# A gate stage in which ScalarE writes the weighted one-hot rows of every eighth unit

## What is computed

```python
v1, i1 = lax.top_k(s1, PEER_TOPK)            # s1, s2: (T, 8 heads, 128 keys)
v2, i2 = lax.top_k(s2, PEER_TOPK)
...
idx = jnp.take_along_axis(cand_idx, pos, axis=-1)    # i1 * 128 + i2: 128 slots for each token
gates = jax.nn.softmax(top_s, axis=-1)
...
u = expert_down[ib]
act = jax.nn.gelu(jnp.einsum("td,thkd->thk", hb, u), approximate=False)
v = expert_up[ib]
return jnp.einsum("thk,thkd->td", gb * act, v)
```

## Time and profile before

| | |
|---|---|
| three runs | 2797.36, 2802.61, 2801.85 us; median 2801.85 |
| profiled execution, own time | 2799.06 us |
| its span, first to last instruction | 2797.4 us |
| PE busy | 2656.8 us (95%) |
| DVE busy | 1807.5 us (65%) |
| ACT busy | 943.0 us (34%) |
| POOL busy | 835.6 us (30%) |
| mean granted TensorE clock | 0.984 of full speed |

### The profile page before, as it was taken

How to read it: one execution, slowest core, us unless ns; L and a number is a source line. 1 busy time by engine, 2 the same in 40 slices (tenths; PEclk the granted TensorE clock), 3 DMA queues, 4 the chain that set the end, 5 groups by cost and what they waited for, 6 DMA issues and landing times.

```text
span 2797.4 us, 35916 instructions
## 1 busy us (share of the span) xinstructions
PE 2656.8 (95%) x12743; PEld 2116.6 (76%) x12743; DVE 1807.5 (65%) x3275; ACT 943.0 (34%) x1219; POOL 835.6 (30%) x542
## 2 busy tenths in 40 slices
PE   4999999999899999999999999999999999899997
PEld 2455445699877899999999887699877877588875
DVE  6752765799999688888888898550128532560532
ACT  2323332333477333223333222443233233332321
POOL 3100011155200144444444322243221234244442
PEclk8999999999999999999999999999999999999999
DMA  9511334333355799999999897223624432122221
GB/s 339 186 57 59 117 141 152 124 123 124 111 198 200 270 336 337 333 334 334 336 341 328 300 309 279 100 83 124 97 90 148 146 120 84 59 98 91 98 90 60
DMA packets 194570, 507.23 MB, mean 181 GB/s; under 512 B 31184, under 2 KB 83184, under 8 KB 192416
## 3 DMA queue, kind: packets, MB, share of 16 engines
q1 hardware_dynamic: 144880, 321.89, 34.6%
q0 software_dynamic: 49584, 184.04, 18.2%
HBM read 456.65 MB, written 49.22 MB: 181 GB/s over the span
## 4 chain that ended last, share of the span: by engine, by line
PE 63%; issue 16%; DVE 12%; POOL 5%; DMA 2%; ACT 1%; DVEq 1%; POOLq 0%; ACTq 0%
PE psum L1668 19%; PE psum L1970 14%; PE psum L1655 13%; PE psum L531 6%; PE psum L546 5%; POOL l_r L878 5%; DVE arena L2018 3%; DVE arena L2015 2%; DVE look_oh L2015 2%; DVE arena L2022 1%; DVEq L2018 1%; PE psum L1977 1%; PE psum L1395 1%; DVE arena L2362 1%; DVE arena L2363 1%
## 5 line engine op out<-in xcount | busy, mean ns | idle before, releaser
L903 ACT ACTIVATE arena<-psum 128x512 f32<-128x512 f32 (+8 forms) x474 | 320.5, 687 | 1102.5 <-PE psum L1655 346.6
L2015 DVE TENSOR_TENSOR arena<-arena 128x384 f32<-128x384 f32 (+8 forms) x399 | 305.7, 772 | 497.3 <-ACT arena L903 269.3
L1668 PE MATMUL psum<-e_r,e_r 128*128 128x512 f32 x2304 | 541.1, 393 | 7.8 <-DVE e_r L2015 7.8
L878 POOL TENSOR_TENSOR l_r<-arena,l_r 128x1024 fp32r<-128x1024 f32 x144 | 351.2, 2440 | 659.6 <-ACT l_r L490 659.6
L1655 PE MATMUL psum<-e_r,e_r 128*128 128x384 f32 x2048 | 534.1, 341 | 3.6 <-ACT arena L903 2.4
L1668 PEld LDWEIGHTS psum<-e_r,e_r 128*128 128x128 f32 x2304 | 434.6, 189 | 97.0 <-issue 4.6
L903 ACT ACTIVATE e_r<-arena 128x1024 fp32r<-128x1024 f32 x256 | 270.2, 1057 | 368.7 <-PE psum L1668 350.1
L1655 PEld LDWEIGHTS psum<-e_r,e_r 128*128 128x128 f32 x2048 | 365.7, 189 | 14.6 <-POOL l_r L848 6.0
L1655 PE MATMUL psum<-e_r,l_r 128*128 128x384 f32 x1024 | 344.6, 337 | 0.0
L862 POOL DMA_INDIRECT arena<-in_down_rows,arena x128 | 160.0, 1250 | 430.8 <-DMA scratch_early<-arena 193.3
L862 POOL DMA_INDIRECT arena<-in_up,arena x128 | 162.0, 1266 | 250.0 <-DVE arena L2499 122.2
(11 more groups left out here) (231 smaller groups left out, 3306.7 us busy)
## 6 DMA issues: line engine op xcount, KB each, us to landing
arena<-in_down SPq DMA_DIRECT2D x128, 512.0 KB
arena<-in_up SPq DMA_DIRECT2D x128, 512.0 KB
arena<-in_w_ada POOLq DMA_DIRECT2D x48, 512.0 KB, 6.8
scratch_gates<-arena SPq DMA_DIRECT2D x12, 2048.0 KB, 7.2
arena<-scratch_gates SPq DMA_DIRECT2D x30, 768.0 KB
arena<-in_w_in SPq DMA_DIRECT2D x44, 512.0 KB, 3.3
arena<-in_w_query SPq DMA_DIRECT2D x16, 512.0 KB, 3.3
arena<-in_w_glu SPq DMA_DIRECT2D x16, 512.0 KB, 3.2
```

Of the source, the lines that this page charges most:

```text
L878: nc.gpsimd.tensor_tensor(rr(lo, 1024, "l"), reg(RING + q % NSLOT * SLOT, 1024), rr(hi, 1024, "l").bitcast(F32), ALU.subtract).then_inc(S[ ...
L903: do(sc.activation(out, in_, f, **kw), sem)
L1668: last = mm(bank(2 * tt_ + hf), rr(w__ + tt_ * P, P), rr(x__ + hf * 512, 512), start=(first and n == 0), stop=(final and n == 2))
L2015: do(v.tensor_tensor(out, a, b, op), sem)
```

## The change

In each chunk the unit with x % 8 == 7 has its B rows written by ACT into a buffer of their own (`small`, columns 96 to 607), in place of DVE. For one token ACT needs two operations: `Abs` of (i2 - iota), and `Relu` of (gate - gate * distance), which is the gate where the distance is 0, and 0 elsewhere since the distance is at least 1 and gates are positive. ACT does one token in each of the four iterations of its loop, ahead of the two copies. The `Abs` has one pointer operand (i2) and ACT waits for its completion; the `Relu` has two (minus the gate as scale, the gate as bias) and signals the new semaphore `b_hotx`, on which PE waits in that unit in addition to what it waited for before. One Copy of 128x48 ahead of the rounds makes the negated gates (`minus_g`). DVE writes A of this unit still; the second half of its chunk is now written out, without a loop. `mag8`, which a later stage uses, moves to other columns of `small`.

```diff
--- before.py
+++ after.py
@@ -129,7 +129,7 @@
     "dve_events": [("pads", 1), ("xr", 8), ("dt_x", 1), ("a_col", 1), ("conv_acc", 12), ("xdt", 8), ("cbm", 2), ("hst", 6),
                    ("ymix", 8), ("xr2", 8), ("hsplit", 1), ("xf_ready", 8), ("gate_lin", 4), ("gd", 1),
                    ("gq", 4), ("ff_split", 32)],
-    "act_6": [("u_hi", 128), ("l_hi", 144)],
+    "act_6": [("b_hotx", 48), ("u_hi", 128), ("l_hi", 144)],
     "pool_1": [("l_lo", 144)],
     "dve_1": [("dte_x", 1), ("sc_free", 4), ("ktok", 4)],
     "dve_2": [("xdte", 3), ("mdec", 16), ("gate_x", 1), ("sm", 4)],
@@ -334,6 +334,8 @@
         assert STG[1] + 4096 <= R0 and SELX + 4 * 384 <= R0
         GB = 2
         OA, OB = UHI, UHI + GB * 512
+        OBX = 96
+        minus_g = small[:, 608:656]
         GATH = PV
         EOUT = PV
         assert GATH + NGATH * 1024 <= R0
@@ -410,7 +412,7 @@
         dtecol = small[:, 352:400]
         a_col = small[:, 400:464]
         dtx, dt_t, dt_2, dt_s = (small[:, 464 + 64 * n:528 + 64 * n] for n in range(4))
-        mag8 = small[:, 256:320]
+        mag8 = small[:, 32:96]
         g_sq, g_mid = gsc[:, 8:16], mod[:, 0:8]
 
         def wslot(s, kt, mcols=P):
@@ -1134,6 +1136,9 @@
             wait("slots_mm", 1)
             for n, at_ in enumerate((I1T, I2T, GT)):
                 act_(reg(at_, TD), bank(n, TD), ACT.Copy, "~slots_T")
+            wait("slots_T", 3)
+            act_(minus_g.rearrange("p (c t) -> p c t", c=NGC),
+                 reg(GT, TD).rearrange("p (c x t) -> p c x t", c=NGC, x=8)[:, :, 7, :], ACT.Copy, scale=-1.0)
 
 
             tn.base["g_evac"] = GB
@@ -1141,7 +1146,11 @@
                 if c >= 2:
                     wait(f"g_stored{c % 2}", 16 * (c // 2))
                 stg = reg(STG[c % 2], GCHUNK * P).rearrange("p (j t) -> p t j", j=P)
-                with tn.loop(8 // GB, g_evac=GB) as i:
+                with tn.loop(8 // GB, g_evac=GB, act_own=1, b_hotx=1) as i:
+                    hot = small[:, bass.ds(i * P + OBX, P)]
+                    act_(hot, con("iota"), ACT.Abs, scale=-1.0, bias=A[:, bass.ds(i + (I2T + 32 * c + 28), 1)])
+                    act_(hot, hot, ACT.Relu, "~b_hotx", scale=small[:, bass.ds(i + (608 + 4 * c), 1)],
+                         bias=A[:, bass.ds(i + (GT + 32 * c + 28), 1)])
                     for u_ in range(GB):
                         wait("g_mm", i * GB + (GB + c * 8 + u_ + 1))
                         act_(stg[:, bass.ds(i * (4 * GB) + 4 * u_, 4), :],
@@ -1687,9 +1696,12 @@
                     r, u_ = x // 8, x % GB
                     pe.wait_ge(S["b_hot"], S.base("b_hot") + i * (8 * NSLOT) + (x + 1))
                     pe.wait_ge(S["g_evac"], S.base("g_evac") + i * (8 * NSLOT) + (x + 1))
+                    if x % 8 == 7:
+                        pe.wait_ge(S["b_hotx"], S.base("b_hotx") + i * (4 * NSLOT) + 4 * (r + 1))
                     for t in range(4):
                         last = mm(bank(u_)[:, t * P:(t + 1) * P], reg(OA + u_ * 512 + t * P, P),
-                                  reg(OB + u_ * 512 + t * P, P), start=True, stop=True)
+                                  small[:, OBX + t * P:OBX + (t + 1) * P] if x % 8 == 7 else reg(OB + u_ * 512 + t * P, P),
+                                  start=True, stop=True)
                     last.then_inc(S["g_mm"], 1)
                     if x % 8 == 0:
                         pe.wait_ge(S["d_loB"], S.base("d_loB") + i * NSLOT + (r + 1))
@@ -2448,16 +2460,29 @@
             low_d(EB)
             wait("slots_T", 3)
             for c in range(2 * NGC):
-                with tn.loop(4 // GB, b_hot=GB) as i:
-                    for u_ in range(GB):
-                        n = 4 * c + u_
-                        wait("g_mm", i * GB + (n + 1))
+                if c % 2 == 0:
+                    with tn.loop(4 // GB, b_hot=GB) as i:
+                        for u_ in range(GB):
+                            n = 4 * c + u_
+                            wait("g_mm", i * GB + (n + 1))
+                            tt(three(OA + u_ * 512, 4, P), bc(con("iota").unsqueeze(1), [P, 4, P]),
+                               bc(A[:, bass.ds(i * (4 * GB) + (I1T + 4 * n), 4)].unsqueeze(2), [P, 4, P]), ALU.is_equal, FREE)
+                            for t in range(4):
+                                ts(reg(OB + u_ * 512 + t * P, P), con("iota"),
+                                   A[:, bass.ds(i * (4 * GB) + (I2T + 4 * n + t), 1)],
+                                   A[:, bass.ds(i * (4 * GB) + (GT + 4 * n + t), 1)], ALU.is_equal, ALU.mult,
+                                   "~b_hot" if t == 3 else FREE)
+                else:
+                    for n in range(4 * c, 4 * c + 4):
+                        u_ = n % GB
+                        wait("g_mm", n + 1)
                         tt(three(OA + u_ * 512, 4, P), bc(con("iota").unsqueeze(1), [P, 4, P]),
-                           bc(A[:, bass.ds(i * (4 * GB) + (I1T + 4 * n), 4)].unsqueeze(2), [P, 4, P]), ALU.is_equal, FREE)
-                        for t in range(4):
-                            ts(reg(OB + u_ * 512 + t * P, P), con("iota"), A[:, bass.ds(i * (4 * GB) + (I2T + 4 * n + t), 1)],
-                               A[:, bass.ds(i * (4 * GB) + (GT + 4 * n + t), 1)], ALU.is_equal, ALU.mult,
-                               "~b_hot" if t == 3 else FREE)
+                           bc(reg(I1T + 4 * n, 4).unsqueeze(2), [P, 4, P]), ALU.is_equal,
+                           "~b_hot" if n % 8 == 7 else FREE)
+                        if n % 8 < 7:
+                            for t in range(4):
+                                ts(reg(OB + u_ * 512 + t * P, P), con("iota"), reg(I2T + 4 * n + t, 1),
+                                   reg(GT + 4 * n + t, 1), ALU.is_equal, ALU.mult, "~b_hot" if t == 3 else FREE)
                 if c % 2 == 0:
                     low_d(EB + c // 2 + 1)
             for n in range(EB + ES + 1, EO):
```

## The result

The changed kernel took 2831.27 us in the median of 4 runs (2824.63 to 2837.56), the kernel before 2802.23 us (4 runs). The ratio is 1.0105, with a 95% interval of 1.0080 to 1.0131: slower by about 1%, where 2829.5 us (2812 to 2838) had been forecast. In a second set of 6 runs the ratio was 1.0079 (1.0063 to 1.0096, median 2826.45 us). The profiled execution took 2827.14 us for a span of 2825.5 us, 28.1 us more than the span of before.

A forecast was written before the change was run, and what follows sets the result against it. DVE was taken to bound the kernel before at 14.16 us per chunk, ACT afterwards at 12.41 + 4 x 1.04 + 0.14 = 16.71. That adds 29.0 us: 2828.1 profiled, 2829.5 us forecast for the median, range 2812 to 2838.

The forecast's parts named there:

- ACT's slack: Gate rounds before the change: ACT has 14.16 - 12.41 = 1.75 us to spare per chunk.
- DVE's 14.16 us per chunk: Gate rounds before the change: DVE bounds, eight units of 1.63 us and one `low_d` of 1.13 us per chunk.
- ACT's 12.41: ACT's own need per chunk before the change, in us, from start distances: 4 x 1.29 + 3 x 1.53 + 2.66.
- ACT's price: Added to each ACT iteration: one Abs and Relu pair, 1.04 us with wait and register instructions, bounds 0.71 to 1.14.
- PE's wait at unit 7: PE's matmuls of unit 7 wait for the fourth Relu, delaying ACT's copy: 0.14 us per chunk.
- The sum: ACT's chunk becomes 12.41 + 4 x 1.04 + 0.14 = 16.71 us; last copy of the rounds 29.0 us later.
- what the change removes: DVE loses four of 32 B operations per chunk, 1.02 us, and would need 13.14 us.
- the rival in which DVE's saving counts: ACT has room in the rounds, so DVE's 12 x 1.02 = 12.2 us go: 2788 us, chance 0.05.
- the point of 0.40 us: Price per Abs and Relu pair on ACT below which a gain was expected: (14.16 - 12.41 - 0.14) / 4.
- Written-out code at nothing: DVE's second half of a chunk without a loop: register instructions already hidden, so worth nothing, at most 0.093 us per operation.
- The cheap pair at 0.71 us: Rival: ACT bounds the rounds but a pair costs only 0.71 us, chunk 15.39 us, 2814 us; chance 0.10.
- fall of the clock: Rival: PE's clock falls in the rounds, half of the units at the lower level, 27 us on top, 2856 us; chance 0.08.

The follow-up runs named there:

- ACT's part alone: Kernel before plus ACT's 48 pairs of Abs and Relu and the negated gates, rows read by nobody, DVE and PE unchanged: 2826.65 us, ratio 1.0083.
- DVE's part alone: Changed kernel without ACT's Abs and Relu and PE's wait for them; PE reads zeros in every eighth unit: 2804.56 us, ratio 1.0003.
- The last two versions: Kernel before, ACT writing one token per second unit, an iteration ahead, copies without own waits: 2794.10 us (0.9972); also DVE's units written out: 2787.72 us (0.9947).
- all units written out: Kernel before, ACT writing one token per second unit an iteration ahead, copies without own waits, DVE's loops written out in both chunk halves: 2787.72 us, ratio 0.9947.
- the spread saving: Kernel before with DVE leaving out one token's B in every second unit, PE multiplying by zeros there, ACT as before: 2793.71 us, ratio 0.9957.

## Why the prediction was right, and where it was not

**The bound of before, and ACT's slack.** DVE's 14.16 us per chunk held. ACT's 12.41 was a little too much: in the chunk of 16.33 us shown above, the steps other than the pairs and the wait at unit 7 add up to 12.23. Two pairs more raise the chunk to 14.25, four to 16.33. That the slack was taken from pitches between starts and not from busy time was right: by busy time the pairs would have fitted in.

**ACT's price.** A pair was put at 1.04 us; it is 0.98 from Abs to copy, plus 0.02 in the gap ahead of it. The two operations cost what was worked out (0.39 and 0.48, measured 0.40 and 0.49); of the two 0.03 us for register instructions only the 0.02 is seen, and the wait between them is 0.18, not 0.20. The two copies of an iteration are 1.26 us apart in place of 1.29.

**PE's wait at unit 7.** 0.14 us was forecast; 1.44 - 1.26 = 0.18 us was measured, and ACT's part alone, without the wait, has the chunk shorter by 16.33 - 16.14 = 0.19.

**The sum.** The chunk was put at 16.71 and is 16.33 us (16.40 in the mean of ten), and the rounds, first copy to last, grew by (943.08 - 748.24) - (916.22 - 747.05) = 25.7 us where 29.0 was forecast. The median shows 29.0 us more and the second set 23.5 us, so the median's agreement to 2 us with the forecast is in part luck. What follows shifted and gave nothing back, as said: from the last copy's start to the end it is 1882.4 us, and was 1881.2.

**The step that was wrong** stands under "what the change removes": that DVE "would need 13.14 us", and so the price of the rival in which DVE's saving counts, 2788 us. DVE's part alone gives 14.0 us and no gain. Bunched in one unit the saving turns into a wait for the buffers; the two-deep ring (`GB` = 2) was described and not followed through. Even spread, the 13.14 was reached only once A had no register instruction behind that wait. The forecast did not rest on it only because ACT's chain was longer still. It does mean that this change, with its saving in one unit, could not have won more than about 12 x 0.15 = 1.8 us at any price of the pair (the rounds of VectorE's part alone are 1.8 us shorter), so the point of 0.40 us that the prediction gave for a gain was without meaning.

**Written-out code at nothing** was right where it stands (ratio 0.9990), and the register instructions of B are hidden as said. The one that can come into the open is A's, which stands behind the wait for PE: where a B less brings DVE up against that wait, writing out is worth about 0.3 us per chunk.

**The rivals.** The cheap pair at 0.71 us did not come, and no fall of the clock within the steady rounds (1.00 from 757 to 945 us). The rule of the Trainium skill (ScalarE: Activation LUTs, Rules for kernel authors) wants relu and multiplications on VectorE; the only size it gives is for bf16. The trace agrees in direction, in f32: 4 x 0.98 us on ACT for 1.02 on DVE. The last two versions show that the rule does not settle the matter when DVE is the bound and ACT has room.

## What to carry to other kernels

Before work is moved to an idle engine, add up its chain by the distances between starts, own waits and branches included, and compare that with the cycle of the engine that bounds: ACT was idle for 53 us ahead of its copies in the rounds and had room for 12 x 1.75 = 21. In a pipeline of two buffers a saving counts only where the consumer can follow it, so take a little from every second unit and not all from one. Put waits of an engine for itself behind other work: without those of the copies the same moved work cost nothing, and spread, issued an iteration ahead and with these waits gone it made the kernel 0.3% faster, 0.5% with VectorE's loops written out as well.

## What the runs showed of the hardware

- Waits of ACT for its own completion are dear in a tight loop: without them on the copies, and with no other edit to the rounds, 48 pairs of ACTIVATEs fitted in (ratio to the kernel before 0.9994 in place of 1.0079; 2802.70 and 2826.45 us, on two chips).
- The same copies of 128x512 from PSUM take 1.065 us in the mean in the changed kernel and 1.083 before. What makes them shorter was not tried.
- In the profiled executions the first copy of the rounds starts between 745.9 us (all units written out) and 756.4 us (the spread saving), although the kernels differ hardly ahead of it. The late ones go with a lower granted clock over the first 300 us: 0.94 with the spread saving and 0.95 with ScalarE's part alone (754.8 us), against 0.97 in the kernel before (747.1) and with all units written out. Why it was lower there is open.
- A register instruction of DVE that stands behind a wait for a semaphore is in the open: A starts 0.15 us behind PE's signal with it (of which it takes 0.076) and as little as 0.02 us without it. Those of B, 0.093 us each, stay hidden with three operations as with four.
